# Streams of the recurrence in one stage with the first layer's projection, in pieces of 256 tokens

## The chip, the cores and the metric

The kernel runs on one core of a Trainium2 chip. The metric is the device time of one execution in microseconds. Five engines work side by side: TensorE (PE) for products, VectorE (DVE), ScalarE (ACT) and GpSimd (POOL) for elementwise work, and SyncE (SP), which here only issues loads. Each engine runs its own instructions in order, and semaphores tie them together.

## The reference

Two layers over 1024 latent tokens and 256 context tokens, width 1024, float32. The first (even) layer has one input projection whose columns feed two mixers: dense attention with 8 query heads and 2 key heads, and a two-direction RWKV-7 recurrence with 8 heads of 64. Cut to what the change touches:

```python
qx, kx, vx, bx, gax, gbx = jnp.split(hx @ w_in, cuts, axis=-1)
p = p + mu * (0.5 * (pp[:, :-2] + pp[:, 2:]) - p)
r, k, v, zw, za = jnp.split(p, ...)
w_log = -softplus(-(w0 + tanh(zw) @ w2)) - 0.5
decay = exp(-exp(w_log));  a = sigmoid(a0 + za @ a2)
kk = k * k_k / max(norm(k * k_k), 1e-12);  kmod = k * (1 + (a - 1) * k_a)
S = S * w_t - (S @ kk_t) b_t + v_t k_t;  y_t = S @ r_t
out = concat(oa * silu(ga), readout(y, r, kmod, v) * silu(gb)) @ w_out
```

The second (odd) layer has the same shape with windowed attention in place of both mixers. Each layer's shift, gain and gate vectors come from `silu(c) @ w_mod + b_mod`.

## The kernel before, in words

The program is a row of stages, each with its own buffers and semaphores: `projected` for layer 0, `decayed_streams`, `chunked_scan`, `attention`, `closing`, then `projected`, `attention`, `closing` for layer 1. A stage ends when all its stores have landed and all engines have met (`Stage.__exit__`, L124 to L128), and only then does the next stage's first load go out.

**`projected`** (L168). First the modulation vectors that this layer needs (L684), then ten tiles of 128 tokens are normed, scaled, turned by TensorE and split into a high and a low part (`first`, `add`, `turn`, `keep_high`, `keep_low`). Then come the products. A job is 128 columns of the weight; its units are the segments of 512, 512 and 256 tokens. Each unit is 24 matmuls (three split products for each of 8 blocks of depth, L164) into one of three accumulators. The list `order` (L199 to L202) is walked by every engine's program with a lag of its own, so that unit i's follow-up stands at i + 1, i + 2 and i + 3 in the others' queues; the first four units are interleaved with the last tiles. A job has a kind:
- gate: ScalarE takes a sigmoid of the accumulator (L387), VectorE multiplies (L582), GpSimd stores.
- mix: ScalarE copies into a padded row (L381); at the job's end GpSimd adds the two neighbours (`neighbours`, L464), VectorE makes the mix (`mix_job`, L589, L592), GpSimd stores a row of `rkvz`.
- rope (queries, keys) and value: norms and rotation on ScalarE, GpSimd and VectorE with two small products (`measure`), or a transposition.

VectorE also splits each job's weights (`split`, L572, L574), two jobs ahead, and SP loads them in the order of the jobs (`load_w`, L346). Layer 0 has 28 jobs: 14 mixes, 1 key, 1 value, 4 queries, 8 gates, in this order.

**`decayed_streams`** (L743). For each of four pairs of heads it reads the rows of r, k and v back from `rkvz` (`load`), over all 1280 tokens at once. Each pair has one norm of the keys (`norm_of`, `clamp`, `unit_keys`) and for each direction: two low-rank products (`loras`, L1057, L1058), two sigmoids on ScalarE (`gates_of`, L869, L873), a scan (L969) and a difference (L973) on VectorE, three exponentials on ScalarE (`exponentials`, L880, L883, L887), seven products on VectorE (`products`, L979 to L995), and one store of 2560 KB on GpSimd's queue (L938). A bonus term (L1000, L1003) and the turned values (L1083) are stored as well. Beside this, TensorE makes the four groups of modulation vectors that later stages need (`mod_sums`, L1071), with `w_mod` loaded by SP in 16 pieces of 1024 KB (L840), and `add_mods` adds the bias.

**`closing`** multiplies the turned mixer output with the stored gate (`multiply`, L2212). `hybrid_layers` (L2297) holds the list of jobs and calls the stages.

## Time and profile before

| | us |
|---|---|
| median of 3 runs | 2613.71 |
| lowest, highest | 2611.72, 2616.97 |
| the profiled execution's own time | 2600.79 |
| its span in the profile | 2599.0 |
| PE busy | 2106.3 (81%) |
| DVE busy | 1252.8 (48%) |
| ACT busy | 825.5 (32%) |
| POOL busy | 697.2 (27%) |
| DMA | 283.12 MB, mean 109 GB/s |

All positions in the trace are counted from the span's start. The profiled execution is one of its own, 0.5% under the median of the timed runs. "Busy" is the time in which an engine had an instruction under way; a matmul's end is modelled, so the distance between two starts tells more of TensorE's rate than the length of one. PEclk is the TensorE clock granted, as a share of full speed (2.4 GHz). A group's row gives line, engine, operation, tiles and forms, count, busy us and mean ns of one, then the idle time in front of the group and what ended it.

### The profile page before, as it was taken

How to read it: one execution, taken by the hardware profiler on the slowest of the kernel's cores; microseconds unless marked ns; L12 is line 12 of the kernel's file. 1: busy time of each engine (PE TensorE's matmuls, PEld its weight loads, DVE VectorE, ACT ScalarE, POOL GpSimd, SP SyncE). 2: the span in 40 equal slices, each digit the busy share in tenths (PEclk: the TensorE clock that was granted, in tenths of full speed). 3: DMA queues.
4: the chain of work that ended last, by engine and by line, in shares of the span. 5: the costliest groups of instructions: out<-in, count | busy, mean ns of one | idle time of the engine just before them, and what ended most of it. 6: DMA issues, size and time to landing. Idle time of an engine off the chain costs nothing. (4 is left out here: it accounts for less than half of the span.)

```text
span 2599.0 us, 59695 instructions
## 1 busy us (share of the span) xinstructions
PE 2106.3 (81%) x26094; PEld 1786.9 (69%) x26094; DVE 1252.8 (48%) x1677; ACT 825.5 (32%) x1393; POOL 697.2 (27%) x737
## 2 busy tenths in 40 slices
PE   3899999644257888888599996794899969999988
PEld 1788878522157777777488886573687758888866
DVE  4344462179534544445344442994546514444422
ACT  2211242065324444444133332222334303333311
POOL 2222472101024232333132000342357523200012
PEclk6899999876679999999899998897899979999989
DMA  7222333278522222221311112654344453211162
GB/s 266 93 91 81 102 95 98 91 292 310 219 76 74 61 88 62 85 65 47 89 65 58 33 36 83 206 167 150 111 114 106 118 134 98 68 49 49 39 200 89
DMA packets 217778, 283.12 MB, mean 109 GB/s; under 512 B 60232, under 2 KB 159208, under 8 KB 215472
## 3 DMA queue, kind: packets, MB, share of 16 engines
q1 hardware_dynamic: 189328, 190.80, 23.8%
q0 software_dynamic: 20688, 81.58, 9.4%
q10 hardware_dynamic: 7504, 6.92, 0.9%
q8 instruction: 208, 3.41, 0.5%
q14 instruction: 50, 0.41, 0.1%
HBM read 191.27 MB, written 87.95 MB: 107 GB/s over the span
## 5 line engine op out<-in xcount | busy, mean ns | idle before, releaser
L164 PE MATMUL in_acc<-in_hi,in_whi 128*128 128x512 f32 (+1 forms) x1024 | 391.7, 382 | 25.0 <-DVE in_lo L565 20.8
L164 PE MATMUL in_acc<-in_lo,in_whi 128*128 128x512 f32 (+1 forms) x1024 | 375.6, 367 | 0.0
L164 PE MATMUL in_acc<-in_hi,in_wlo 128*128 128x512 f32 (+1 forms) x1024 | 375.5, 367 | 0.0
L164 PEld LDWEIGHTS in_acc<-in_hi,in_whi 128*128 128x128 f32 x1024 | 196.2, 192 | 63.5 <-issue 31.8
L164 PEld LDWEIGHTS in_acc<-in_lo,in_whi 128*128 128x128 f32 x1024 | 196.2, 192 | 36.9 <-issue 7.2
L164 PEld LDWEIGHTS in_acc<-in_hi,in_wlo 128*128 128x128 f32 x1024 | 195.8, 191 | 31.9
L1845 DVE TENSOR_REDUCE dense_top<-dense_score 128x1 f32<-128x640 f32 (+1 forms) x144 | 112.3, 780 | 162.4 <-PE dense_score L1932 162.4
L1845 DVE TENSOR_REDUCE window_top<-window_score 128x1 f32<-128x640 f32 (+1 forms) x128 | 101.3, 791 | 185.0 <-PE window_score L1928 185.0
L1970 PEld LDWEIGHTS dense_outs<-dense_V,dense_p 128*128 128x128 f32 x1344 | 169.8, 191 | 8.5 <-ACT dense_p L1813 5.0
L1970 PE MATMUL dense_outs<-dense_V,dense_p 128*128 128x65 f32 x1344 | 170.0, 270 | 0.9 <-ACT dense_p L1813 0.8
L1970 PE MATMUL window_outs<-window_V,window_p 128*128 128x65 f32 x1216 | 158.8, 274 | 1.6 <-ACT window_p L1813 1.1
L1970 PEld LDWEIGHTS window_outs<-window_V,window_p 128*128 128x128 f32 x1216 | 151.2, 193 | 8.9 <-ACT window_p L1813 2.6
L1366 DVE TENSOR_TENSOR scan_X<-scan_X,scan_small 128x512 f32<-128x512 f32 x80 | 55.0, 688 | 180.8 <-PE scan_small L1494 179.4
L1499 PE MATMUL scan_wide<-scan_XT,scan_Y 64*64 64x64 f32 x3200 | 120.4, 224 | 22.4 <-issue 22.4
L164 PE MATMUL close_acc<-w_hi,close_hi 128*128 128x512 f32 x288 | 118.0, 410 | 17.7 <-DVE close_lo L2218 17.7
L1813 ACT ACTIVATE dense_p<-dense_turned 128x512 f32<-128x512 f32 x168 | 96.2, 597 | 108.3 <-PE dense_turned L1956 107.9
L1475 PE MATMUL scan_small<-scan_X,scan_off 64*64 64x64 f32 x3200 | 120.0, 227 | 9.2 <-issue 8.0
L2144 POOL MEMSET close_eps<- 128x1 f32 x2 | 0.2, 104 | 467.7 <-POOLq L127 467.7
L1244 POOL TENSOR_TENSOR scan_DG<-scan_LB,scan_lmask 128x512 f32<-128x512 f32 x20 | 25.3, 1266 | 372.7 <-ACT scan_LB L1280 372.7
L1499 PEld LDWEIGHTS scan_wide<-scan_XT,scan_Y 64*64 64x64 f32 x3200 | 106.8, 136 | 25.2 <-issue 25.2
L1253 POOL TENSOR_TENSOR scan_off<-scan_LA,scan_lmask 128x512 f32<-128x512 f32 x100 | 124.0, 1276 | 0.0
L1475 PEld LDWEIGHTS scan_small<-scan_X,scan_off 64*64 64x64 f32 x3200 | 110.0, 142 | 14.9 <-issue 13.9
(257 smaller groups left out, 4946.6 us busy)
## 6 DMA issues: line engine op xcount, KB each, us to landing
streams<-decay_out POOLq DMA_DIRECT2D x8, 2560.0 KB, 9.1
scan_L<-streams SPq DMA_DIRECT2D x80, 256.0 KB, 3.6
decay_wm<-in_w_mod SPq DMA_DIRECT2D x16, 1024.0 KB, 9.0
in_raw<-in_w_in_even SPq DMA_DIRECT2D x28, 512.0 KB, 3.6
in_raw<-in_w_in_odd SPq DMA_DIRECT2D x20, 512.0 KB, 3.8
close_ga<-gates SPq DMA_DIRECT2D x18, 512.0 KB, 4.5
in_wm<-in_w_mod SPq DMA_DIRECT2D x8, 1024.0 KB, 12.3
gates<-in_outs POOLq DMA_DIRECT2D x32, 256.0 KB, 2.3
```

Source lines behind the costliest of these rows:

```text
L164: last = pe.matmul(out, a(k), b(k), start=(k == 0 and x == 0), stop=(k == n - 1 and x == 2))
L1244: pool.tensor_tensor(DG[:], LB[:], lmask[:, 0:1, :].to_broadcast([P, NU, HD]), ALU.mult).then_inc(diagonal, 1)
L1253: pool.tensor_tensor(off[s][:, k], triangles, lmask[:, k + 1:k + 2, :].to_broadcast([P, NU, HD]), ALU.mult).then_inc(off_done, 1)
L1366: dve.tensor_tensor(X[s][:], X[s][:], small[s][:], ALU.subtract).then_inc(x_less[s], 1)
L1475: return pe.matmul(small[s][half_of(1 - c), u, :], off[s][half_of(c), k, u, :], X[s][half_of(c), u, :], start=True, stop=True)
L1499: return pe.matmul(wide[s][half_of(1 - c), u, :], Y[s][half_of(1 - c), u, :], XT[j % 3][half_of(1 - c), u, :], start=True, stop=True)
L1813: act.activation(p[:, s % NP_], turned[s % NTURN][:], ACT.Exp, scale=SCALE).then_inc(expd, 1)
L1845: dve.tensor_reduce(top[:, i % NSLOT, x, r:r + 1], score[:, :, 0:width], AXS, ALU.max).then_inc(topped, 1)
L1970: last = pe.matmul(outs[i % 2][:, r * HW:(r + 1) * HW], p[:, s % NP_, r * P:(r + 1) * P], v, start=(k == 0 and r == 0), stop=(k == n - 1 a ...
L2144: pool.memset(eps[:, 0:1], EPS).then_inc(readied, 1)
```

## The change

`decayed_streams` is removed, and `projected` does its work for layer 0.

- Order of jobs: two gates, key, value, four queries, then the 14 mixes (the two low-rank rows first, then key, receptance and value row of each pair), then six gates.
- The list `items`: for each pair five key pieces ("N") and ten pieces ("X": five pieces of 256 tokens x two directions). A table says which pieces stand behind which unit: from unit 40, one per unit for five units, then 1.35 per unit. Each engine handles piece t in slot t and what follows it in slot t + 1; there are 61 slots, the last of them behind the last unit.
- Streams in pieces: sigmoid(x) becomes 0.5 tanh(x/2) + 0.5 everywhere, for the rates with a second ScalarE instruction. In both layers the gate's sigmoid is a tanh, the factor 0.5 is applied in `closing`.
- Modulation for later stages: 32 steps of one 512 KB load (issued by ScalarE, three buffers) and four matmuls, one behind each element of `order` from the seventh on.
- GpSimd stores 512 KB per piece and direction; SP loads r, k, v of a piece in one transfer, two buffers. SP's loads are sorted by the unit behind which they may go.
- Buffers of the tile phase and of the heads are given up to those of the streams (`early.close()`), with GpSimd's `clear` in between.

```diff
+    LATE_AT, NWL, QW = 6, 3, D // 4
+    SG = 256
+    NSG, PT = TOK // SG, SG // P
+    items = [x for b in range(PAIRS) for x in [("N", b, s) for s in range(NSG)] + [
+        ("X", b, s, d) for s in range(NSG) for d in range(2)]] if decay else []
+    CLEAR_AT, N_AT = 36, 40
...
+    for u in range(NU + 5):
+        slot_of_unit[u] = min(len(items) + 1, max(0, min(u - N_AT, NSG) + max(0, (u - N_AT - NSG) * 27 // 20)))
...
+                    if t == 5:
+                        for g, (lay, col) in enumerate(LATE):
+                            for q in range(4):
...
+                def load_rkv(q):
...
+                    if q >= 2:
+                        sp.wait_ge(bon_done, q - 1)
+                        sp.wait_ge(values_in, q - 1)
+                    sp.dma_start(rkv[:, q % 2], rkvz[b:b + 2 * PAIRS + 1:PAIRS, :, c0:c0 + SG].rearrange("c p n -> p c n")
+                                 ).then_inc(rkv_in[q % 2], 16)
...
-                        act.activation(to, src, ACT.Sigmoid).then_inc(sig, 1)
+                        act.activation(to, src, ACT.Tanh, scale=0.5).then_inc(sig, 1)
...
+                def rates(b, s, d):
...
+                    act.activation(rate[:, h], aux[:, h, 0:SG], ACT.Tanh, scale=0.5, bias=w0h[:, d, b:b + 1]).then_inc(rate_t, 1)
+                    act.wait_ge(rate_t, n + 1)
+                    act.activation(rate[:, h], rate[:, h], ACT.Identity, scale=0.5, bias=halves[:]).then_inc(rate_done, 1)
...
+                    act.activation(sigs[:, h], aux[:, 2 + h, 0:SG], ACT.Tanh, scale=0.5, bias=a0h[:, d, b:b + 1]).then_inc(sig_done, 1)
+                def exponentials(b, s, d):
...
+                    act.wait_ge(subtracted, n + 1)
+                    if n >= 1:
+                        act.wait_ge(r_done, n)
+                        act.wait_ge(totals, n)
+                    act.activation(e_to[:], cum[:, h], ACT.Exp, scale=-DECAY).then_inc(exp_to, 1)
+                    act.activation(before[:, h], before[:, h], ACT.Exp, scale=-DECAY).then_inc(exp_in, 1)
+                    act.wait_ge(exp_to, n + 1)
+                    act.activation(cum[:, h], cum[:, h], ACT.Exp, scale=DECAY).then_inc(exp_from, 1)
...
+                def slot(t):
...
+                    if item(t - 1)[0] == "X":
+                        exponentials(*item(t - 1)[1:])
+                        if item(t - 1)[3] == 1:
+                            values_out(*item(t - 1)[1:3])
+                    if item(t)[0] == "X":
+                        rates(*item(t)[1:])
...
+                    pool.dma_start(streams[d][b][:, s * PT:(s + 1) * PT], streams_out[:, d]).then_inc(s_stored[d], 16)
...
+                def slot(t):
...
+                    if item(t)[0] == "N":
+                        clamp(*item(t)[1:])
+                    if item(t)[0] == "X":
+                        sums(*item(t)[1:])
+                    if item(t - 1)[0] == "N":
+                        unit_keys(*item(t - 1)[1:])
+                    if item(t - 1)[0] == "X":
+                        products(*item(t - 1)[1:])
+                        if item(t - 1)[3] == 1:
+                            bonus_of(*item(t - 1)[1:3])
...
+                def late_sums(g, k):
+                    m = g * KC + k
+                    pe.wait_ge(wl_in[m % NWL], (m // NWL + 1) * 16)
...
+                    for q in range(4):
+                        last = pe.matmul(side[32 * q:32 * q + 32, 0:QW], sl[:, k, :], wl[:, m % NWL, q * QW:(q + 1) * QW],
+                                         start=(k == 0), stop=(k == KC - 1))
...
+                def slot(t):
...
+                    if item(t)[0] == "X":
+                        loras(*item(t)[1:])
...
-                    dve.tensor_tensor(ga[:, s], tr[:], ga[:, s], ALU.mult).then_inc(multiplied, 1)
+                    dve.scalar_tensor_tensor(ga[:, s], ga[:, s], 0.5, tr[:], ALU.mult, ALU.mult).then_inc(multiplied, 1)
...
+    blocks = [NFC - 2, NFC - 1] + [x for b in range(PAIRS) for x in (PAIRS + b, b, 2 * PAIRS + b)]
+    gates = gate_jobs(GA, gates0, 3)
+    jobs0 = (gates[:2] + key_jobs(QC, AKV, kst0) + value_jobs(QC + AKV * HD, AKV, v0) + query_jobs(0, AH, qst0, 3) + mixes
+             + gates[2:])
```

The new `products` has the seven VectorE products of the old one on 256 tokens, in the order b, mixed key, key times mix, r, kk, b times, k times; r, the store's buffer and the rates are awaited there. The new `sums` is the old scan and difference.

## Rows read from the trace of the kernel before

**Rows 1.** Windows: us; busy and count of five engines; granted clock; DMA share, GB/s.

```profile
295.00:497.00 202.00, 201.55 (x1011) 166.92 (x1009) 84.50 (x121) 54.57 (x103) 84.86 (x120) 1.00 0.32 91
504.00:689.00 185.00, 66.84 (x416) 33.12 (x416) 146.56 (x102) 98.06 (x85) 16.09 (x30) 0.68 0.73 272
701.00:1275.00 574.00, 445.28 (x16880) 416.74 (x16880) 255.72 (x420) 229.25 (x420) 173.87 (x140) 0.92 0.24 71
```

**Rows 2.** Timeline at the two stage borders: start us, length, engine, line.

```profile
497.87 0.54 POOL L505 DMA_DIRECT2D gates<-in_outs  x1 [1.85 <-DVE in_outs L582]
503.59 0.37 SPq L818 DMA_DIRECT2D decay_kkc<-in_kk_b  x1
...
687.40 1.55 DVE L1003 SCALAR_TENSOR_TENSOR decay_bon<-decay_rkv,decay_rkc,decay_bon 128x1280 f32<-128x1280 f32 x1
701.30 0.35 SPq L1190 DMA_DIRECT2D scan_ident<-in_consts  x1
```

**Rows 3.** TensorE's timeline: three unit starts, lora products, late sums of four steps.

```profile
479.82 0.28 PE L164 MATMUL in_acc<-in_hi,in_whi 128*128 128x256 f32 x1
482.70 0.40 PE L164 MATMUL in_acc<-in_hi,in_whi 128*128 128x512 f32 x1
488.16 0.39 PE L164 MATMUL in_acc<-in_hi,in_whi 128*128 128x512 f32 x1
...
570.32 0.38 PE L1057 MATMUL decay_odd<-decay_tz,decay_w2s 64*128 64x256 f32 x1
570.54 0.38 PE L1057 MATMUL decay_odd<-decay_tz,decay_w2s 64*128 64x256 f32 x1
570.88 1.93 PE L1071 MATMUL decay_acc<-decay_wm,sl 128*32 128x256 f32 x32
```

**Rows 4.** VectorE in the streams' stage: groups (count, busy us, mean ns), two timeline rows.

```profile
L969 DVE TENSOR_TENSOR_SCAN decay_cum<-decay_carry,decay_rate 128x1280 f32<-128x1280 f32 x8 | 22.6, 2822 | 12.4 <-ACT decay_rate L869 12.4
L982 DVE TENSOR_SCALAR decay_km<-decay_sig,decay_kac,decay_kan 128x1280 f32<-128x1280 f32 x8 | 7.5, 942 | 0.0
...
549.29 1.48 DVE L993 TENSOR_TENSOR decay_out<-decay_km,decay_e_from 128x1280 f32<-128x1280 f32 x1
550.69 1.48 DVE L995 TENSOR_TENSOR decay_out<-decay_kk,decay_e_in 128x1280 f32<-128x1280 f32 x1
```

**Rows 5.** Groups by form of VectorE in the projection.

```profile
L574 DVE TENSOR_TENSOR in_wlo<-in_raw,in_whi 128x1024 fp32r<-128x1024 f32 x26 | 56.7, 2181 | 0.9
L592 DVE SCALAR_TENSOR_TENSOR in_mix<-in_near,in_half,in_mix 128x1282 f32<-128x1282 f32 x14 | 22.7, 1620 | 2.7 <-POOL in_near L464 2.3
L572 DVE CAST in_whi<-in_raw 128x1024 fp32r<-128x1024 f32 x26 | 20.2, 776 | 94.3 <-PE in_acc L164 94.3
...
L589 DVE TENSOR_SCALAR in_mix<-in_pad,in_keep 128x1282 f32<-128x1282 f32 x14 | 12.3, 878 | 0.0
L582 DVE TENSOR_TENSOR in_outs<-in_acc,in_xs 128x512 f32<-128x512 f32 x16 | 11.1, 691 | 62.5 <-ACT in_xs L387 62.5
L612 DVE TENSOR_TENSOR in_ls<-in_ho,in_hs 128x256 fp32r<-128x256 f32 x5 | 2.1, 418 | 2.8 <-ACT in_hs L417 2.8
```

**Rows 6.** Groups by form of ScalarE in the projection and the streams' stage.

```profile
L403 ACT ACTIVATE in_work<-in_work 128x256 f32<-128x256 f32 x5 | 2.1, 418 | 0.2
...
L869 ACT ACT_TABLE_LOAD x8 | 10.3, 1283 | 1.9 <-ACT decay_tot L892 1.8
L880 ACT ACT_TABLE_LOAD x8 | 10.3, 1283 | 6.4 <-DVE decay_out L988 6.3
L898 ACT ACTIVATE decay_tz<-decay_tz 128x1280 f32<-128x1280 f32 x1 | 1.3, 1269 | 15.5 <-DMA decay_tz<-rkvz 15.5
```

**Rows 7.** Group of GpSimd's neighbour sums in the projection.

```profile
L464 POOL TENSOR_TENSOR in_near<-in_pad 128x1282 f32<-128x1282 f32 x14 | 33.9, 2420 | 103.9 <-ACT in_pad L381 97.7 <-DVE in_mix L592 6.2
```

**Rows 8.** DMA issues of both stages: count, KB each, median us to landing.

```profile
streams<-decay_out POOLq DMA_DIRECT2D x8, 2560.0 KB, 9.1
rkvz<-in_mix POOLq DMA_DIRECT2D x14, 512.0 KB, 2.9
```

More of the change, by code:

```diff
@@ L263, in projected @@
             wm_in = st.sems(*(f"wm_in{k}" for k in range(KC)))
+        mix_jobs = [j for j, job in enumerate(jobs) if job["kind"] == "mix"]
         if mu is not None:
@@ L349, in _ @@
+                for _, _, load, args in sorted(loads, key=lambda x: x[:2]):
+                    load(*args)
             @block.scalar
@@ L434, in _ @@
+                if LATE:
+                    for m in range(NWL):
+                        load_late(m)
                 for what, i in order:
+                    g, k = late(index_of[what, i] - 1)
+                    if g is not None and k < KC and g * KC + k + NWL < len(LATE) * KC:
+                        load_late(g * KC + k + NWL)
                     if what == "T":
@@ L445, in _ @@
                         go_on(i - 2)
+                    for t in slots(what, i):
+                        slot(t)
+                if decay:
+                    act.wait_ge(values_stored, PAIRS * NSG * 16)
+                    for d in range(2):
+                        act.wait_ge(tot_stored[d], PAIRS * 16)
             @block.gpsimd
@@ L513, in _ @@
                 for what, i in order:
+                    g, k = late(index_of[what, i])
+                    if k == KC:
+                        store_late(g)
+                    if decay and what == "U" and i == CLEAR_AT:
+                        clear()
                     if what == "T":
@@ L648, in _ @@
                 for what, i in order:
+                    g, k = late(index_of[what, i])
+                    if k == KC:
+                        add_late(g)
                     if what == "T":
@@ new lines, in _ @@
+                    else:
+                        if i < NU:
+                            product(i)
+                        if is_kind(i - 1, "rope"):
+                            measure(i - 1)
+                        if is_kind(i - 1, "value"):
+                            turn_back(i - 1)
+                    g, k = late(index_of[what, i])
+                    if k is not None and k < KC:
+                        late_sums(g, k)
+                    for t in slots(what, i):
+                        slot(t)
```

681 lines of the change are left out of this document (332 added, 349 removed).

## The prediction

> **What bounds it now.** I read the windows first, cut at the stage borders. The first layer's projection is bound by TensorE in its second half: 201.55 of 202 us busy, clock 1.00, while VectorE is busy for 84.50 and ScalarE for 54.57 [rows 1]. The stage behind it, decayed_streams, is the other way round: VectorE is busy for 146.56 of 185 us, TensorE for 66.84, at clock 0.68 [rows 1]. The two stand in a row, with their openings and drains. The timeline at the borders gives 497.87 for the projection's last store, 503.59 for the first load of the streams' stage, 688.95 for the end of its last VectorE instruction and 701.30 for the scan's first load [rows 2]. So the streams' stage costs 701.30 - 503.59 = 197.7 us. The change lays it beside the projection, whose free engines are those it needs. The question is what the joined stretch is bound by.
>
> **Order and counts.** There are 28 jobs of three units (512, 512, 256 tokens), so 84 units. The streams become 60 pieces of 256 tokens: 20 for the keys, 40 for (pair, piece, direction), 5 from unit 40 on and then 1.35 for each unit. The last are issued behind unit 83. Units 40 to 83 are two units and 14 jobs.
>
> **TensorE.** A unit of 256 tokens takes 482.70 - 479.82 = 2.88 us, one of 512 takes 488.16 - 482.70 = 5.46 us [rows 3]. A job is 13.8 us, the joined stretch 14 x 13.8 + 8.3 = 201.5 us. The window from 295 has 201.55 busy us [rows 1], so TensorE's last product ends at about 496.7, and unit 40 starts at 496.7 - 201.5 = 295.2 us now. New in the stretch are 40 pairs of 256-column lora products at 2 x 0.215 us (starts 570.32, 570.54 [rows 3]; the second projection runs beside the first) = 17.2 us, 20 sums of squares of the same 0.43 us = 8.6, and 40 transposes, at most 0.2 us each by the same rate and 0.12 as I take them = 4.8. That is 30.6, and TensorE's need is 232 us.
>
> **Ahead of unit 40.** The late modulation sums: 32 steps; 32 records, four steps, lie in 1.93 us [rows 3], so 0.48 us a step, about 16 us in all, on TensorE's path. Their loads (32 of 512 KB) move from SP's queue to ScalarE's. ScalarE is idle there most of the time (busy 54.57 of 202 us in the window with the queries [rows 1]), so issuing and the wait in front of each are hidden; without that cover the read of a product would come 0.9 us later per unit, inside the three accumulators' slack. The 16 bias loads on SP stand ahead of three tiles' loads and cost at most 7 us, if those tiles were needed at once. Gates come first, so four sigmoid-like reads now fall between the square roots of the token tiles: up to four table loads of 1.28 us [rows 6]. For both, and for ScalarE waiting on the late sums between tiles, I take 5 us (bounds 0 and 12). Unit 40 then starts at 295.2 + 16 + 5 = 316 us. The opening of the old stage, its drain and its five-fold larger stores go.
>
> **VectorE in the stretch.** For 256 tokens a product of two SBUF operands is 0.42 us (L612 [rows 5]); back to back the next starts 0.08 us before the end (549.29, 550.69 against a length of 1.48 us [rows 4]). The scan: 2.82 us for 1280 [rows 4] is 0.15 fixed and 2.09 ns a column, so 0.68 us. The mixed key 0.41. One (piece, direction) is the scan, a difference, two factors and the five products: 0.68 + 0.41 + 7 x 0.42 = 4.03, less five overlaps, plus small gaps = 3.7 us; 40 of them are 148 us. A key piece has four at 0.42 to 0.48: 1.84 us, 20 are 37. The bonus is 0.93 us, 20 are 18.6. Together 204 us, where whole rows took 147: pieces cost the fixed part five times. The projection's own work there: nine mix jobs with split 0.78 + 2.18 and mix 0.88 + 1.62 [rows 5] = 49; four more splits, not slowed, of 1.9 = 7.6; gates 12 x 0.69 + 6 x 0.42 = 10.8. That is 67.5, and VectorE's need is **271 us**, more than TensorE's 232. So VectorE, not TensorE, sets the stretch.
>
> **The loop.** A second limit is the ring between ScalarE and VectorE. The exponentials of a piece wait for the r product of the one before, the rates of the next stand behind them on ScalarE, the scan waits for the rates, and the next r product stands behind the scan. By 0.42 us for 256 columns on ScalarE [rows 6], the ScalarE half is three exponentials, totals, half of a value copy and its store's issue, tanh and the scaling: 2.55 us. The VectorE half from scan to r product is 2.7 us. The ring is 5.25 us, VectorE works 3.7 + 0.46 of it, so 1.1 us is idle for each of 40 pieces, 44 us, where no split, mix or gate falls into the gap. About 18 pieces have such work in front; I take 25 us idle (bounds 0 and 60). The end of VectorE: 316 + 271 + 25 = 612 us.
>
> **Queues.** GpSimd gets 40 stores of 512 KB and 20 of the bonus, 0.55 us each = 33 us, beside nine sums of neighbours at 2.42 us [rows 7]: about a quarter busy. A store has to land before the same direction's next product, about 9 us after it is ready; 0.55 + 2.9 us (the store of 512 KB [rows 8]) fits. SP's weight loads now queue behind loads that wait for a bonus, but are issued four units before use and land in about 3 us (as many bytes [rows 8]): hidden, at the price of 3 us a job if VectorE fell four units behind. VectorE's 12.35 us from last instruction to the scan [rows 2] hold a landing of about 9.1 us (2560 KB [rows 8]); with 2.9 us about 6 us are left. The closing's gate product takes the half as a second scalar: at most 0.06 us x 18, nothing.
>
> **The sum.** The scan starts at 612 + 6 = 618 us instead of 701.3: -83 us. The profiled execution took 2600.8 us (span 2599.0), so 2518 on its terms. The runs shown have the median 2613.7, 0.5% above it; I put the same 83 us off that: **2531 us**.
>
> **GpSimd against VectorE.** L574 takes 2.18 us where 0.15 + 1.05 ns x 1024 gives 1.22 [rows 5]; it runs beside the 2.42 us neighbour sums [rows 7]. The sum holds this as 9 x 0.96 = 8.6 us. The Trainium skill ("SBUF — State Buffer", section "SBUF: two separate sides") says that a VectorE instruction with two SBUF inputs and a GpSimd one exclude each other for a whole instruction. By that each neighbour sum would cost its full 2.42 us, now that nearly all of VectorE's work has two SBUF inputs: 21.8 us, 13 us more, 2544.
>
> **Rivals.**
> - *TensorE stays the bound.* If VectorE's small pieces are cheaper than I price them or the projection's work fills every gap, TensorE's 232 us count: 548, then the last three or four pieces at 5.25 us and the exit, 571 us for the scan: -130, **2484**. For it: VectorE is under half busy in the stretch now. Against: the row sums above. Chance 0.12.
> - *More idle in the stretch.* TensorE needs 232 of 296 us, so it pauses. The scan stage, with 445 of 574 us busy, has clock 0.92 [rows 1]. Products grow only where the mean clock falls below 232/296 = 0.78; the old streams' stage had 0.68 at 36% busy. A mean of 0.7 gives 331 us. Or a store lands in 9.1 us as now [rows 8], 0.6 us late for 40 pieces, 26 us. The one gives 35 us more, both 61: **2557 to 2592**, and 2600 with the tile phase at its bound. Chance 0.16.
> - *Slower: the tables.* Each sigmoid batch beside exponentials loads a table now, 8 times before sigmoid and 8 before exp, 1.28 us each [rows 6]. The change writes sigmoid as tanh. If tanh and exp still need different tables, each of 40 pieces gets both loads inside the ring, between exponentials and rates: 40 x 2.57 = 103 us, scan at 721, **2634**. It decides from 83/40 = 2.1 us a piece. For it: no row shows tanh after exp. Against: tanh (L898) ran behind the gates' sigmoids with no load of its own, and squares (L403) have none either [rows 6], so functions share tables. Chance 0.07. The Trainium skill ("ScalarE: Activation LUTs", section "Table sets: the hidden batching unit") lists tanh in exp's set; by that the loads are gone but for the switches at the keys' reciprocal roots, and this rival is dead. No run here shows it yet.
> - *No effect.* Stretch and streams still follow each other because some in-order wait holds all: 2608 to 2619. Chance 0.03. Other ways to be slower, 0.02.
>
> **Chances.** The main case (VectorE and the ring) has 0.60 and its own range 2506 (no idle) to 2566 (60 idle). With the neighbours from both sides, 2484 to 2600 holds about 8 in 10. Runs differ by 5 us, 0.2%, about what a measurement of this kernel can tell. Faster by more 0.88, within 0.03, slower 0.09.
>
> **What would show it.** In the new profile: no streams' stage; scan's first load near 618; late steps of about 0.48 us ahead of unit 40; in the stretch VectorE over 85% busy, TensorE near 80%, its waits put down to VectorE or ScalarE; scan of 256 near 0.68 us and products near 0.42; a ring of about 5.2 us from r product to r product; table loads only around the key pieces and gates. Wrong, if TensorE is over 97% busy up to unit 83 (first rival), if its clock is under 0.8 (second), or if a table load stands before each tanh (third).

## The result, and the profile after

The change makes the kernel faster, by far less than forecast. The forecast was 2531 us, 83 below the median shown; measured is a median of 2584.6 us (four runs, 2581.4 to 2589.6) against 2615.3 us of the kernel before on the same chip: ratio 0.9886, interval 0.9846 to 0.9925, 31 us less. A second measurement, later, gave 2565.4 against 2597.9 us, ratio 0.9881 (0.9860 to 0.9902). The measured ratios in this text are estimates over the runs of both kernels on one chip; they differ from the quotient of the two medians by up to 0.0015. The profiled execution took 2581.4 us, span 2579.6.

The timeline at the border between the joined stage and the scan, in the changed kernel (start us, length, engine, line):

```profile
657.61 0.48 DVE L1001 SCALAR_TENSOR_TENSOR in_bon<-in_rkv,in_rkc,in_bon 128x256 f32<-128x256 f32 x1
...
658.39 0.55 POOL L772 DMA_DIRECT2D bonus<-in_bon  x1
672.38 0.34 SPq L1284 DMA_DIRECT2D scan_ident<-in_consts  x1
```

The scan's first load stands at 672.4 instead of 701.3 [rows 2], 28.9 us earlier; forecast was 618. What lies behind it took 1907.2 us against 1897.7. That difference is scatter of the scan, which no part of the change touches: it took 574.4 us before, 584.0 in the changed kernel and 570.2 when that kernel was profiled again, and 568.8 to 583.9 in the other kernels below with no order to it. The stretch before the scan repeats better. Unaltered, the changed kernel gave 671.9 the second time; the kernel of e10 gave 641.3 and 641.1; the kernel of e11 gave 663.7 and 667.1. So the experiments are read at this border, the medians are a check, and differences under 4 us in end or border are taken as scatter.

Why 658 and not 612 for VectorE's end? The windows of the joined stretch in the changed kernel, cut at the first scan instruction (L961) of each group of ten pieces and at the last one's start, show it. Columns: window; its length; busy us of PE, PEld, DVE, ACT, POOL; granted clock; DMA share; GB/s. The first row and every second one after it are key sections (five key slots and what stands around them), the others groups of pieces; the last ends with VectorE:

```profile
322.00:353.40 31.40, 31.40 (x163) 26.52 (x162) 16.50 (x29) 14.91 (x28) 7.90 (x6) 1.00 0.34 114
353.40:409.10 55.70, 45.57 (x235) 35.37 (x233) 48.29 (x95) 27.62 (x78) 15.66 (x18) 0.91 0.53 168
409.10:437.50 28.40, 23.08 (x100) 18.38 (x101) 18.01 (x40) 11.69 (x26) 6.66 (x8) 0.82 0.47 161
437.50:494.70 57.20, 45.99 (x226) 34.54 (x224) 51.60 (x96) 27.28 (x78) 16.45 (x19) 0.92 0.52 169
494.70:524.40 29.70, 24.47 (x120) 20.28 (x121) 20.96 (x43) 14.39 (x28) 7.21 (x9) 0.81 0.45 151
524.40:570.60 46.20, 40.85 (x204) 31.33 (x203) 40.86 (x96) 26.25 (x76) 9.12 (x18) 0.96 0.60 189
570.60:605.60 35.00, 28.94 (x128) 23.62 (x126) 20.20 (x45) 21.50 (x36) 4.81 (x9) 0.85 0.36 117
605.60:658.10 52.50, 24.42 (x131) 17.69 (x129) 43.21 (x108) 26.69 (x78) 10.40 (x20) 0.75 0.48 161
sum 336.10, PE 264.71 PEld 207.74 DVE 259.62 ACT 170.33 POOL 78.21; mean PE 33.09 PEld 25.97 DVE 32.45 ACT 21.29 POOL 9.78
```

In each row, length less DVE busy is VectorE's idle time. The four groups of pieces have 7.4 + 5.6 + 5.3 + 9.3 = 27.6 us of it. The four key sections have 14.9 + 10.4 + 8.7 + 14.8 = **48.8 us**, and the forecast gave them none. TensorE, at 201.55 of 202 in the projection alone [rows 1], is idle for 71 of these 336 us. Its granted clock is 0.75 in the last row, where it idles most (28 of 52.5 us), and 0.81 to 0.96 in the six before. VectorE's waits in the stretch (us in total, times, longest):

```profile
DVE in_cum L961 <- ACT in_rate L604: 29.4, 26, 2.0
DVE in_norm L938 <- PE in_side L1132: 29.2, 14, 4.5
DVE in_outs L857 <- ACT in_xs L523: 11.1, 4, 4.0
DVE in_norm L944 <- ACT in_ksq L594: 0.9, 1, 0.9
```

The first is the ring of the pieces. The second is VectorE waiting in the key slots for the keys' sums of squares, the third for the gates' reads, the fourth for ScalarE's square of the root. Added up by window, the 48.8 us of the key sections are 29.2 of the second, 11.1 of the third, 5.7 of the first, 0.9 of the fourth and 1.9 in gaps under 0.15 us.

The third has a cause of its own. All 17 table loads of ScalarE in this stretch lie in the key sections, 8 of them in the last, where gates' reads (tanh) stand between the keys' roots:

```profile
595.31 1.28 ACT L592 ACT_TABLE_LOAD   x1
...
597.49 1.28 ACT L523 ACT_TABLE_LOAD   x1
598.79 0.39 ACT L523 ACTIVATE in_xs<-in_acc 128x256 f32<-128x256 f32 x1
...
599.20 0.42 DVE L857 SCALAR_TENSOR_TENSOR in_outs<-in_xs,in_acc 128x256 f32<-128x256 f32 x1 [3.99 <-ACT in_xs L523]
```

So VectorE waits 4.0 us for a gate of 0.4 us, and two loads lie in that time. Durations came out as forecast: the scan of 256 columns and the table loads in groups of the stretch (line, engine, operation, count, busy us, mean ns, idle before):

```profile
L961 DVE TENSOR_TENSOR_SCAN in_cum<-in_carry,in_rate 128x256 f32<-128x256 f32 x40 | 31.3, 783 | 29.4 <-ACT in_rate L604 29.4
L849 DVE TENSOR_TENSOR in_wlo<-in_raw,in_whi 128x1024 fp32r<-128x1024 f32 x13 | 23.6, 1816 | 0.5
L592 ACT ACT_TABLE_LOAD x8 | 10.3, 1283 | 1.6 <-ACT in_vt_out L635 1.5
L523 ACT ACT_TABLE_LOAD x5 | 6.4, 1283 | 0.1
L602 ACT ACT_TABLE_LOAD x3 | 3.8, 1283 | 0.1
L644 ACT ACT_TABLE_LOAD x1 | 1.3, 1283 | 0.0
```

An undisturbed scan takes 0.69 us (0.68 forecast), the products 0.42.

### The profile page after: what moved, and what is told of

Its sections match the earlier page's. It is cut to its first block and busy times, and to the rows that moved or that the text cites. A ratio compares the mean times of both kernels' runs of the same rounds, so it can differ in the third digit from the quotient of the medians.

```text
span 2579.6 us, 61157 instructions
## 1 busy us (share of the span) xinstructions
PE 2130.2 (83%) x26174; PEld 1790.7 (69%) x26174; DVE 1292.5 (50%) x2064; ACT 871.7 (34%) x1685; POOL 722.2 (28%) x786
## 5 line engine op out<-in xcount | busy, mean ns | idle before, releaser
L164 PE MATMUL in_acc<-in_hi,in_whi 128*128 128x512 f32 (+1 forms) x1024 | 400.6, 391 | 19.6 <-DVE in_lo L840 17.6
L1338 POOL TENSOR_TENSOR scan_DG<-scan_LB,scan_lmask 128x512 f32<-128x512 f32 x20 | 25.3, 1266 | 382.9 <-ACT scan_LB L1374 382.9
L1569 PE MATMUL scan_small<-scan_X,scan_off 64*64 64x64 f32 x3200 | 119.9, 226 | 11.2 <-issue 10.4
L1388 ACT ACTIVATE scan_Y<-scan_small 128x512 f32<-128x512 f32 x100 | 59.7, 597 | 189.8 <-PE scan_small L1569 189.8
```

Of the source, the lines that this page charges most:

```text
L164: last = pe.matmul(out, a(k), b(k), start=(k == 0 and x == 0), stop=(k == n - 1 and x == 2))
L1338: pool.tensor_tensor(DG[:], LB[:], lmask[:, 0:1, :].to_broadcast([P, NU, HD]), ALU.mult).then_inc(diagonal, 1)
L1388: act.activation(Y[s][:], small[s][:], ACT.Copy).then_inc(y_read[s], 1)
L1569: return pe.matmul(small[s][half_of(1 - c), u, :], off[s][half_of(c), k, u, :], X[s][half_of(c), u, :], start=True, stop=True)
```

## The experiments

All are edits of the changed kernel. "End" is the end of VectorE's last instruction of the joined stage, "border" the scan's first load. The unaltered kernel has end 658.1 and border 672.4. Idle times are VectorE's, added up over windows cut as above. The last column is the ratio of the times to the kernel before on the same chip; it is empty where there is one run only.

| kernel | end | border | VectorE busy from 322 | idle in key sections | idle in groups | ratio |
|---|---|---|---|---|---|---|
| forecast | 612 | 618 | 271 (from 316) | 0 | 25 | 0.968 |
| changed kernel | 658.1 | 672.4 | 259.6 | 48.8 | 27.6 | 0.9886 |
| e1_ring | 637.1 | 651.4 | 259.9 | 44.8 | 10.4 | 0.9803 |
| e5_cost | 656.3 | 671.9 | 266.6 | 38.0 | 29.7 | |
| e6_ring_cost | 640.3 | 655.9 | 266.3 | 37.3 | 14.7 | 0.9823 |
| e10_dense_own | 634.0 | 641.3 | 264.3 | 31.6 | 16.1 | 0.9752 |
| e12_no_squares | 642.1 | 656.4 | 261.8 | 30.5 | 27.7 | |
| e13_two_passes | 642.5 | 656.8 | 260.5 | 33.8 | 26.2 | |

**The ring: e1_ring.**

```diff
-            e_to, b_, bon = (st.sb(n, [P, SG]) for n in ("e_to", "b_", "bon"))
+            b_, bon = (st.sb(n, [P, SG]) for n in ("b_", "bon"))
+            e_to = st.sb("e_to", [P, 2, SG])
...
-                    if n >= 1:
-                        act.wait_ge(r_done, n)
-                        act.wait_ge(totals, n)
-                    act.activation(e_to[:], cum[:, h], ACT.Exp, scale=-DECAY).then_inc(exp_to, 1)
+                    if n >= 2:
+                        act.wait_ge(r_done, n - 1)
+                        act.wait_ge(totals, n - 1)
+                    act.activation(e_to[:, h], cum[:, h], ACT.Exp, scale=-DECAY).then_inc(exp_to, 1)
...
```

> The changed kernel with the factor e_to in two halves, so that the exponentials of a piece no longer wait for the r product of the one before. Theory A (the ring of ScalarE and VectorE over the one e_to sets a piece at about 5.2 us, and the units' mixes and splits are added to it): VectorE's period inside a group of pieces falls from 5.2 to about 4.2 us, its last instruction comes at 658 - 40 x 1.1 = 614 us or somewhat before, and the time is 40 to 45 us lower than that of the changed kernel, about 2542. Theory B (the order of the slots sets it: groups of 10 pieces on VectorE's side, key slots in between on TensorE's): the groups of pieces get shorter as in A, the 28 to 35 us between them stay. Theory C (VectorE's own sum of work sets it): period and end hardly move, under 10 us gained. Theory D (a store that lands late): the wait moves from the rates to the stores of streams_out, under 15 us gained.

Measured: end 637.1, 21 us earlier, half of what theory A expected; median 2559.8 us, ratio 0.9803 (0.9748 to 0.9859). The idle time in the groups fell from 27.6 to 10.4 us, that of the key sections only from 48.8 to 44.8. That is theory A's mechanism inside the groups, with the stretches between them at 26.6 to 32.6 us, as theory B had it. So the ring was real and of the forecast's size (25), and it was not where the missing 46 us were. VectorE's waits in this kernel, the key slots' on top:

```profile
DVE in_norm L939 <- PE in_side L1133: 25.3, 13, 4.5
DVE in_cum L962 <- ACT in_rate L605: 12.1, 15, 2.0
```

**The order of the slots: e2_order and e4_ring_order** (the second with e_to in two halves as well).

```diff
-    items = [x for b in range(PAIRS) for x in [("N", b, s) for s in range(NSG)] + [
-        ("X", b, s, d) for s in range(NSG) for d in range(2)]] if decay else []
+    keys = [("N", q // NSG, q % NSG) for q in range(PAIRS * NSG)]
+    items = keys[0:NSG] if decay else []
+    for q in range(PAIRS * NSG if decay else 0):
+        between = [keys[q + NSG - 2]] if 2 <= q <= (PAIRS - 1) * NSG + 1 else []
+        items = items + [("X", q // NSG, q % NSG, 0)] + between + [("X", q // NSG, q % NSG, 1)]
```

> The changed kernel with the key slots of pair b + 1 laid one at a time between the two directions of pair b's pieces instead of five in a row; nothing else changes, e_to stays single. Theory B (phases add up because the engines can only be some two units apart): key work falls into the gaps of the ring, TensorE has no stretch at 100% and none at 50%, VectorE's last instruction comes 30 to 40 us earlier than 658, the time is about 2550. Theory A alone (the ring sets it, whatever the order): 20 key slots still cost their 2 us on VectorE, and what the ring takes stays: 0 to 15 us gained. Theory C: no gain.

> Both edits, e_to in two halves and the key slots laid between pieces. If A and B both hold, VectorE is bound by its own work: 322 + 271 (the need as predicted, 260 by the busy time that the profile of the changed kernel shows) + some 5 = 590 to 600 us for its last instruction, 58 to 68 us before 658, time about 2520 to 2527. If only one holds, the result is that of its own kernel within 5 us. If TensorE's 265 busy us at a mean clock of 0.88 bound it, the end is near 322 + 245 = 567 plus the last pieces, and VectorE has idle time that ends on TensorE.

Measured: ends at 653.7 and 643.7, medians 2567.2 and 2566.5 us (ratios 0.9842 and 0.9829). The first, 4.4 us earlier, is what theory A alone expected. The second is worse than the ring's edit alone (637.1), so none of its theories' numbers came. VectorE's wait for the sums of squares fell to 13.0 us (25.3 in e1), and its wait for the rates rose to 38.1 us (12.1 in e1). In front of the rates stand ScalarE's table loads, 33 in the stretch instead of 17, because each key slot now sits alone between exponentials and needs the reciprocal root's table, and the next tanh needs the other one back. ScalarE's table loads in e4_ring_order:

```profile
L596 ACT ACT_TABLE_LOAD x16 | 20.5, 1283 | 1.6 <-ACT in_tot L628 1.4
L606 ACT ACT_TABLE_LOAD x11 | 14.1, 1283 | 0.2
L527 ACT ACT_TABLE_LOAD x5 | 6.4, 1283 | 0.1
L648 ACT ACT_TABLE_LOAD x1 | 1.3, 1283 | 0.0
```

That is 16 x 1.28 = 20.5 us more on ScalarE, inside the ring. Laying the keys between the pieces trades the key sections' waits for these loads, by the trace; no kernel has this order without the loads.

**Slots dealt out by cost: e5_cost, e6_ring_cost, e7_ring_cost_start.** The order stays, only the table of slots per unit changes (e7 also has `CLEAR_AT, N_AT = 35, 38` and 41 for 42):

```diff
-    for u in range(NU + 5):
-        slot_of_unit[u] = min(len(items) + 1, max(0, min(u - N_AT, NSG) + max(0, (u - N_AT - NSG) * 27 // 20)))
+    spent, budget, done = 0.0, 0.0, 0
+    for u in range(NU + 5 if decay else 0):
+        while done < len(items) + 1 and u > N_AT and spent < budget and (done < NSG or u > 42):
+            spent += 1.9 if done < len(items) and items[done][0] == "N" else 4.1
+            done += 1
+        slot_of_unit[u] = done
+        if u >= N_AT:
+            budget += 4.2 if u < 66 else 5.2
```

> The changed kernel with another table of slots per unit, e_to single as before: slots are dealt out by VectorE's cost (1.9 us for a key slot, 4.1 for a piece; 4.2 us of it per unit before unit 66, 5.2 behind it), so that five key slots lie in two units and ten pieces in seven to nine. No slot changes its place in the order, so no table load is added. Theory B (phases add up): the 28 to 35 us between the groups of pieces fall to some 15, the groups stay at the ring's pace of 5.2 us with the mixes on top; VectorE's last instruction 15 to 25 us before 658. Rival (only the ring or VectorE's sum counts, not how slots lie against units): 658 within 5 us.

> The same table of slots, and e_to in two halves as in e1_ring. Theory B with A: groups of pieces at VectorE's own pace (about 52 us with mixes, 40 without), 12 to 15 us between them: VectorE's last instruction near 590, 45 us before that of e1_ring (637), the time about 2515. If TensorE then bounds it (265 busy us at the clock it gets): 585 to 600 as well, but with VectorE's waits put down to TensorE. Rival (the order against units does not matter): 637 within 5 us, 2560.

> As e6_ring_cost, and slot 0 stands at unit 38 instead of 40 (the clearing one unit earlier, the first piece from unit 41): two units of 4.6 us more for the same work. If VectorE's work bounds the stretch, its end comes 6 to 10 us before that of e6_ring_cost; if TensorE does, the end is the same within 3 us.

Measured: ends at 656.3, 640.3 and 641.5. Against the same kernel without the new table (658.1 and 637.1) that is nothing, as the rival had it: theory B's 45 us did not come. The windows say why. The key sections lost 10.8 and 7.5 us of idle time, but the groups gained 2.1 and 4.3, and VectorE's busy time grew by 6.4 to 7 us, because all nine of GpSimd's neighbour sums now fall on VectorE's two-operand work, against six (last section). And 37 us of idle time stayed in the key sections, with TensorE idle there for 36 to 39 us, where it was 17 in the changed kernel. e7 starts the first piece 2.9 us earlier (343.9 against 346.8) and ends no earlier, which speaks against VectorE's work as the bound; it does not tell what held it.

**What holds the key sections: e9_dense, e10_dense_own, e12_no_squares, e13_two_passes.** One key slot passes over four engines: ScalarE squares, TensorE sums, VectorE clamps, ScalarE takes the root and squares it, VectorE refines; and the next slot's square writes the tile (`ksq`) that the refinement still reads. e9 is e8_drain (below) with all five key slots of a pair in one unit; e10 is e9 with a tile of its own for the halved square:

```diff
-                        act.wait_ge(refined_k, q - 1)
...
-                    act.activation(ksq[:, q % 2], root[:, q % 2], ACT.Square, scale=0.5 ** 0.5).then_inc(halved_k, 1)
+                    act.activation(hsk[:, q % 2], root[:, q % 2], ACT.Square, scale=0.5 ** 0.5).then_inc(halved_k, 1)
```

> As e8_drain, with all five key slots of a pair in one unit, so that no product of TensorE lies between them. In the traces of the changed kernel and of e6_ring_cost VectorE waits 29.2 and 24.6 us for the keys' sums of squares (L1132 in the first), which TensorE runs behind a unit's product or behind the loop of the keys (clamp, refinement on VectorE, the next squares on ScalarE, the sums on TensorE: 3.2 us from clamp to clamp where nothing else lies between). Theory E (the keys' waits are what is left of the phases): with the product gone from between them the loop's 3.2 us stand against 1.85 us of VectorE's own work, 16 x 1.35 = 22 us of waits stay, and VectorE's end moves little: 635 to 640 (640 in e8_drain). Rival (the product in between was the cost): waits for the sums under 10 us, end near 625.

> As e9_dense, with a tile of its own for the halved square of the root, so that the next squares of keys on ScalarE no longer wait for the refinement of those before. Theory E: the keys' loop is open, VectorE's wait for the sums of squares falls from some 25 us to under 8, its last instruction comes at 618 to 625 instead of 640, the scan's first load at 626 to 633 instead of 647.5, and the time is about 2530. Rival (whatever VectorE gains at the keys it waits for TensorE's products behind them, because TensorE has 232 us of work of its own and loses clock whenever it pauses): end at 635 to 640 as before, with the waits moved to the rates (lora products) and the gates.

Measured: e9 ended at 650.6, 10 us later than e8_drain (640.1), outside both expectations; the wait for the sums hardly moved (22.3 us). e10 ended at 634.0: the wait for the sums fell to 5.6 us, 16.7 less than in e9, and the end came 16.6 us earlier than e9's. So the wait for the sums was opened as theory E had it, but the end is not at its 618 to 625: against e8_drain only 6 us are gained, since part of the wait moved on, much as the rival had it (635 to 640). Why e9 alone lost 10 us is not shown; its waits for the rates were 25.1 us against 18.4 in e8, and 7.7 us for accumulators are new. VectorE's waits in e10:

```profile
DVE in_cum L970 <- ACT in_rate L611: 26.6, 15, 5.1
DVE in_whi L856 <- PE in_acc L164: 7.0, 3, 2.9
DVE in_norm L947 <- PE in_side L1141: 5.6, 3, 4.5
```

The timeline of e10 behind a key section shows where the first line comes from:

```profile
511.24 0.48 PE L1151 MATMUL in_aux<-in_tz,in_w2s 64*128 64x256 f32 x1
...
511.98 0.47 ACT L609 ACTIVATE in_rate<-in_aux,in_w0h 128x256 f32<-128x256 f32 x1 [4.32 <-PE in_aux L1151]
512.48 0.51 ACT L611 ACTIVATE in_rate<-in_rate,in_halves 128x256 f32<-128x256 f32 x1
513.02 0.69 DVE L970 TENSOR_TENSOR_SCAN in_cum<-in_carry,in_rate 128x256 f32<-128x256 f32 x1 [3.12 <-ACT in_rate L611]
```

The first piece's lora product stands behind two units' products on TensorE (501.4 to 511.2), and these stand behind the last sum of squares (500.72); ScalarE waits 4.3 us for it and VectorE 3.1 us for ScalarE. Here TensorE's order makes the other two wait in turn.

Two kernels that leave work out ask how much of this is TensorE's load. e12 leaves out the keys' sums of squares (VectorE's clamp reads ScalarE's square instead); e13 leaves out one of the three split products of every block in units 40 to 83:

```diff
-                    dve.tensor_scalar(norm[:, q % 2], side[:, 0:SG], 1e-24, None, ALU.max).then_inc(clamped, 1)
+                    dve.tensor_scalar(norm[:, q % 2], ksq[:, q % 2], 65536.0, None, ALU.max).then_inc(clamped, 1)
...
```

```diff
-                                   lambda k: hi[:, k, t0:t0 + n], lambda k: lo[:, k, t0:t0 + n]).then_inc(summed, 1)
+                                   lambda k: hi[:, k, t0:t0 + n], lambda k: lo[:, k, t0:t0 + n], passes=2 if decay and u >= 40 else 3).then_inc(summed, 1)
...
```

> The changed kernel without the keys' sums of squares: TensorE leaves out those 20 products of 0.43 us, and VectorE's clamp reads ScalarE's square from SBUF instead of their sum from PSUM (with a floor of 65536, so that the values stay small). Only the wait of VectorE for TensorE in the key slots is gone (29.2 us in the trace of the changed kernel); order, slots, the single e_to and all other work stay. Theory W (that wait is a cost of its own): VectorE's last instruction comes 20 to 29 us earlier than 658. Theory B (in the key slots TensorE's products are the bound, and VectorE's wait is only where it shows): VectorE meets TensorE at the next thing that it needs from it, the lora products of the first piece of each group; the wait moves there (rates, L961 <- L604, and ACT L602 <- PE L1142), and the end moves by less than 10 us.

> The changed kernel, with one of the three products of each weight tile (low half of the weights by high half of the tokens) left out for units 40 to 83: TensorE has a third less of the projection to do there, and nothing else changes. Theory B (the key slots are bound by TensorE's products, the pieces by VectorE and the ring): the key slots' period falls from 5.8 us to the keys' own loop of some 3.2 to 4 us, the gaps between the groups of pieces from 28 to 35 us to 18 to 22, the groups themselves stay at 46 to 57 us, and VectorE's last instruction comes 25 to 40 us before 658. Rival (the waits of VectorE in the key slots come from the keys' own loop over three engines, not from TensorE's load): end within 10 us of 658. If the groups shrink as well, TensorE had a hand in them too.

Measured: ends at 642.1 and 642.5, 16 us before 658.1 in both. e12 lies between its two theories: 29 us of waits were taken away, of which 16 reached the end. What is left in its key sections, 30.5 us, has the same 11.1 us for the gates. e13 leaves the sums in and takes work from TensorE. Its windows, laid as above:

```profile
322.00:345.60 23.60, 22.12 (x113) 18.11 (x112) 16.78 (x29) 14.42 (x27) 7.91 (x6) 1.00 0.44 147
345.60:399.80 54.20, 35.57 (x170) 26.53 (x168) 48.25 (x97) 27.43 (x78) 15.68 (x18) 0.80 0.55 174
399.80:425.10 25.30, 19.22 (x76) 14.86 (x77) 18.61 (x40) 11.72 (x26) 6.67 (x8) 0.75 0.52 179
425.10:482.30 57.20, 36.19 (x162) 25.56 (x160) 51.60 (x96) 27.30 (x78) 16.48 (x19) 0.84 0.51 169
482.30:511.80 29.50, 23.09 (x97) 18.31 (x98) 21.02 (x44) 14.44 (x28) 7.23 (x9) 0.74 0.45 151
...
590.00:642.50 52.50, 20.85 (x88) 13.77 (x88) 43.20 (x108) 26.71 (x78) 10.42 (x20) 0.66 0.48 161
sum 320.50, PE 209.63 PEld 156.51 DVE 260.47 ACT 169.73 POOL 78.35; mean PE 26.20 PEld 19.56 DVE 32.56 ACT 21.22 POOL 9.79
```

TensorE is busy for 209.6 instead of 264.7 us, 55 less, and the end moves by 15.6. Three of the four groups of pieces keep their lengths to the tenth (57.2, 46.2 and 52.5 us), and the first loses 1.5 us, though TensorE's clock there is 0.66 to 0.85: it has next to no hand in them. The key sections shrink from 124.5 to 110.4 us, 7.8 of it in the first, where TensorE had been busy without a break, and 33.8 us of idle time stay in them. The wait for the sums of squares fell from 29.2 to 15.7 us, the one for the gates stayed at 11.1. So a third of the products was worth 15 of the 48.8 us. Theory B, whose 25 to 40 us did not come, and its rival, by which the end stays within 10 us of 658, both fall. The two thirds of the products that are left in e13, at a lower clock, still stand between the sums; so 15 us is a lower bound of TensorE's share, and how the rest divides between it and the chain from engine to engine is open. No kernel here brought the key sections' idle time under 30 us.

**The exit: e3_sems, e8_drain, e11_drain_alone.** From VectorE's end to the scan's first load it is 14.3 us, where 6 were forecast. e3 has 30 unused semaphores more; e8 is e6, and e11 the changed kernel, with two drains of GpSimd in the middle of the stage:

```diff
+        spare = st.sems(*(f"spare{a}" for a in range(30 if decay else 0)))
```

```diff
+                    if decay and what == "U" and i in (62, 80):
+                        pool.drain()
```

> The changed kernel with 30 more semaphores allocated in the joined stage, which nothing uses; they are cleared with the others when the stage ends. Theory: the longer exit (last data at 661, the scan's first load at 672.4, 11.3 us, against about 4 us at the two exits of the kernel before) is the clearing of about 120 semaphores instead of about 70 and 50; by that slope of about 0.14 us each the exit becomes 15 to 16 us. Rival (the exit waits for something else: the end of a late write, code of the next stage being fetched): 11 us as before, within 1 us.

> As e6_ring_cost, with a drain of GpSimd at units 62 and 80, where nothing waits for GpSimd. The trace of the changed kernel has a GpSimd DRAIN of 9.38 us at the end of the joined stage (2.35 us at the end of each of the two stages before, with 121 and 28 transfers issued by GpSimd; 0.87 and 0.71 us in the closing stages with 10 and 8). Theory: a drain costs about 0.08 us for each transfer that GpSimd has issued since something last tidied them, so the one at the exit falls under 1.5 us, the exit from 14.0 to about 6 us, and the time by 8 us against e6_ring_cost. Rival: the drain at the exit has another cause and stays 9.4 us; the two added ones only delay stores.

> The changed kernel with nothing but a drain of GpSimd at units 62 and 80. Theory (the exit's length is the last drain's): the drain at the exit falls from 9.38 to about 1.1 us as in e8_drain, the scan's first load comes 5.7 us after the last store's issue plus landing, at about 664 instead of 672.4, and the time is 8 us lower than that of the changed kernel (0.3%): about 2576. Rival (the two drains, 5.5 us each, hold GpSimd's stores up and VectorE behind them): VectorE's last instruction moves from 658 to beyond 663.

Measured: in e3 the time from the last store's issue to the border was 14.2 us against 14.0, so the semaphores are not it, and the rival held. The trace has what is: GpSimd's DRAIN at the end of the stage. The rows of one line's instructions give the count, the duration in ns as least, median and most, and the first and last start in us. First the kernel before, its streams' stage and its two closing stages:

```profile
L803 POOLq DRAIN  x1: 2345/2345/2345, 698.0 to 698.0; - x1
...
L2045 POOLq DRAIN  x2: 706/788/869, 1786.6 to 2597.5; - x2
```

Then the changed kernel (the joined stage, and layer 1's projection with 1686 ns):

```profile
L380 POOLq DRAIN  x2: 1686/5531/9376, 661.5 to 2092.3; - x2
```

And e8_drain, its exits (again with layer 1's 1686) and its two added drains:

```profile
L387 POOLq DRAIN  x2: 1106/1396/1686, 644.9 to 2056.8; - x2
L808 POOLq DRAIN  x2: 5502/5514/5527, 479.4 to 619.3; - x2
```

The drain took 9.38 us in the changed kernel, with all transfers landed before it began, and 1.11 us in e8, whose border came 8.4 us before e6's (647.5 against 655.9) with the same VectorE end; its median was 2545.4 us, ratio 0.9731 (0.9645 to 0.9818), against 2565.9 in e6. The interval in e6 is 0.9754 to 0.9891, so the medians do not separate these two; the border does. In e11 the drain took 1.60 us, and the border stood at 663.7 with VectorE's end at 657.2, so the exit was 6.5 us instead of 14.3; its median, 2569.7 us at a ratio of 0.9883 (0.9859 to 0.9908), did not show that gain. At the exits of stages GpSimd had issued 8, 10, 14, 20 and 28 transfers since the drain before when the drain took 0.71, 0.87, 1.11, 1.60 and 2.35 us: about 0.08 us each. The two added drains took 5.5 us each in e8, 7.0 and 5.7 in e11, of a GpSimd that is a quarter busy.

**Side by side: e14_changed_again, e15_all_again, e16_drain_again.**

> The changed kernel once more, unaltered, so that the next two can be set against it on the same chip: 25 to 36 us below the kernel before.

> The kernel of e10_dense_own once more (e_to in two halves, slots by cost with the key slots in one unit, own tile for the halved square, GpSimd's drains): 31 us before the changed kernel at the scan's first load, so 28 to 38 us below it in time, 1.1 to 1.5%.

> The kernel of e11_drain_alone once more, beside the changed kernel: 8.7 us earlier at the scan's first load; if nothing takes that back behind it, 6 to 11 us less in time than the changed kernel.

| on one chip | median us | ratio to before | interval |
|---|---|---|---|
| kernel before | 2597.9 | | |
| e14, the changed kernel | 2565.4 | 0.9881 | 0.9860 to 0.9902 |
| e16, with the two drains | 2561.3 | 0.9862 | 0.9834 to 0.9891 |
| e15, everything of e10 | 2531.8 | 0.9751 | 0.9723 to 0.9778 |

e15 beats both kernels: 33.6 us under the changed one, as expected, and the intervals are apart. The drains alone gave 4.1 us, under the 6 to 11 expected, with intervals that overlap; in the profiled execution of e16 VectorE ended 3 us later than in e14 (660.6 against 657.7), so its border (667.1 against 671.9) shows 4.8 us, where e11's had shown 8.7. Of these 3 us, 1.7 were there when unit 40 began (323.3 against 321.6), ahead of both drains. That the drains shorten the exit is shown, twice from 14.3 to 6.5 us; that the whole of it reaches the median is not.

## Why the forecast was right in direction and wrong in size

- *What the change does.* Right: the streams run beside the projection, no opening or exit of their own, and VectorE's chain sets the end. TensorE alone is not the bound: it is idle for 71 of 336 us, and e13 takes 55 us of work from it for 16 us at the end. So the first rival is dead.
- *Ahead of unit 40.* Forecast 316, measured 322. The late sums took more than 0.48 us a step: 224 records, 28 steps, took 18.0 us, 0.64 each, 20.6 us for 32 steps instead of 16. A step by itself takes 0.64 us where four in a row took 1.93 together [rows 3], and the forecast had taken a quarter of the row.
- *VectorE's need.* Forecast 271, measured 259.6 us busy, 11 less. Scan and products had their forecast prices; without collisions the 40 pieces took 139 us for 148 (some 4 of the 9 are short gaps that the forecast had counted as work), the keys 33 for 37, and GpSimd's neighbour sums cost 5 us more than forecast. VectorE is busy for 77% of the stretch, not over 85%.
- *The ring.* Forecast 25 us of idle time, measured 27.6 in the groups of pieces, and e1 took 17 of them away. Its mechanism holds as well. From scan to scan it is 4.8 and 5.6 us in turn where only the bonus or nothing stands between, 5.2 in the mean as forecast; the longer of the two has 2.1 us idle. Where a split or a mix stands between, 0.1 to 0.3 us stay idle (1.6 in the first interval): the unit's work fills the gap. The intervals of 8.6 to 9.1 us each hold a mix or a split and a collision with GpSimd (last section).
- *The step that failed.* "VectorE works 3.7 + 0.46 of it, so 1.1 us is idle for each of 40 pieces": the loop was drawn for the 40 pieces alone, and the 20 key slots went into the sum as 37 us of VectorE's work with no wait at all. The sections in which they stand carry **48.8 us** of idle time: 29.2 for the keys' sums of squares, which TensorE runs behind units' products, and 11.1 for gates whose tanh stands between the keys' roots. The windows then add up to 322 + 259.6 + 27.6 + 48.8 = 658.0, as they must. Against 612 that is + 6 - 11.4 + 2.6 + 48.8 = + 46. That the wait for the sums costs time is shown by e12 (without it the end comes 16 us earlier) and by e10 against e9 (16.7 us less wait, 16.6 us earlier).
- *More idle in the stretch.* The late store did not occur: it landed in 3.8 us at the median. The granted clock was 0.88 over the stretch, above this rival's 0.8, and by e13 it is no term in the groups. In the key sections it can be a part. There TensorE's products of 512 columns start 0.43 us apart at first and 0.23 later, as in the second:

```profile
418.34 0.63 PE L164 MATMUL in_acc<-in_lo,in_whi 128*128 128x512 f32 x1
418.77 0.63 PE L164 MATMUL in_acc<-in_hi,in_wlo 128*128 128x512 f32 x1
...
423.52 0.39 PE L164 MATMUL in_acc<-in_lo,in_whi 128*128 128x512 f32 x1
423.75 0.39 PE L164 MATMUL in_acc<-in_hi,in_wlo 128*128 128x512 f32 x1
```

  By such starts the products of the last three key sections took some 8 us longer than at the full rate (an estimate from the trace); how much of it VectorE waited for, no run separates. This rival's time, 2557 to 2592, held the result, but mainly for another reason, the waits in the key slots; that is luck.
- *The exit.* Forecast 6 us, measured 14.3. Landing was as forecast; GpSimd's drain went from 2.35 to 9.38 us. The forecast had read the old exit as landing plus a rest, and did not ask what the rest depends on. This is a second term that was too small, by 8 us.
- *The tables.* Dead: L602, the tanh of each piece, ran 40 times with 3 loads. By this the rule of the Trainium skill ("ScalarE: Activation LUTs", section "Table sets: the hidden batching unit"), that tanh stands in exp's set, agrees. The loads that are left, at the keys' roots and the gates between them, were named in the forecast and priced at nothing; some of them lie in the 11.1 us above, and e4 has 16 more of them.
- *The sum.* Border 618 forecast, 672.4 measured: + 46 and + 8. Against before that is -28.9 where -83 was forecast, and the medians say -31 and -32.5.

## What to carry to other kernels

When one stage is laid beside another, every kind of slot needs its own loop drawn over all engines, the cheap kind as well: here the sections of 20 slots with under 2 us of work each held 48.8 us of idle time (37.7 without the gates' waits), the groups of 40 heavy ones 27.6. Sum the bound engine's work and its waits section by section: dealing the slots out evenly (e5, e6) did not even out what stood in the sections. And at a stage's exit read each engine's drain in the trace; two placed early shortened the exit by 8 us, and no profile shows them holding VectorE by more than the scatter of the stretch.

## What the runs showed of the hardware

**GpSimd and VectorE.** Nine neighbour sums ran in the stretch, and six of them fell on a two-operand instruction of VectorE. Such pairs in the timeline of the changed kernel:

```profile
438.20 2.32 POOL L700 TENSOR_TENSOR in_near<-in_pad 128x1282 f32<-128x1282 f32 x1 [7.94 <-ACT in_pad L517]
438.24 2.56 DVE L963 TENSOR_TENSOR in_before<-in_cum,in_rate 128x256 f32<-128x256 f32 x1
...
465.29 4.07 DVE L849 TENSOR_TENSOR in_wlo<-in_raw,in_whi 128x1024 fp32r<-128x1024 f32 x1
...
465.93 2.34 POOL L700 TENSOR_TENSOR in_near<-in_pad 128x1282 f32<-128x1282 f32 x1
```

A difference of 0.42 us took 2.56 us, a split of 1.22 us took 4.07: VectorE lost 2.1 us to a neighbour sum of 2.3, and 2.8 us in the second pair. The six cost 2.1, 1.9, 1.9, 2.0, 2.8 and 2.8 us, 13.6 before rounding, where the forecast's mean from rows had 8.6. In e10 eight did, at 19.1 us, and in e5 and e6 all nine, at 21.1 and 21.6 us, which is most of what the slots by cost gave back. The rule of the Trainium skill ("SBUF — State Buffer", section "SBUF: two separate sides"), that the two exclude each other for a whole instruction, agrees: in each of the six pairs VectorE's instruction ended only after GpSimd's, 0.3 to 1.1 us behind it. The 21.8 us that the forecast worked out by it for nine are what e5 and e6 show (21.1 and 21.6), and the changed kernel's 13.6 are six collisions. So what decides is how many of them collide.

**GpSimd's drain.** At a stage's exit, with GpSimd's own work done and landed, it took about 0.08 us for each transfer that GpSimd had issued since the last drain, when these were few (8 to 28). With 121, 122 and 197 it took 2.35, 1.69 and 9.38 us, so the count alone does not give it; what else does, no run here shows. The drains put in the middle do not follow that rate: with 138 or 139 and with 39 or 44 transfers issued and stores still under way they took 5.3 to 7.0 us.
